# Expert stage of a two-block layer: hidden rows turned by VectorE in 32x32 blocks, places spread by one product, sums stored in 2 or 4 KB pieces

## Chip, core and metric

The kernel runs on one core of one Trainium2 chip. A core has five engines that run beside each other: TensorE (PE, with its weight loads as PEld), VectorE (DVE), ScalarE (ACT), GpSimd (POOL) and SyncE (SP, which here only issues loads). 16 DMA engines move data between DRAM and the on-chip memory. The metric is the device time of one execution in microseconds (us), the median over runs; less is better.

## What is computed

A first block (attention of two kinds, then a mixture of experts) and a second block (differential attention and retention), for 512 tokens of 1024 float32 values. Only the mixture of experts is touched by the change. Cut to what matters it is

```python
logits = (hf @ router_w + router_b)                  # 512 tokens, 32 experts
top_val, top_idx = lax.top_k(logits, 4)              # each token goes to 4 experts
gate = jax.nn.softmax(top_val, axis=-1)
# for the rows (tokens) of one expert e:
u = hf[toks] @ w1[e] + b1[e]                         # w1[e]: 1024 x 2048
g_, lin = u[:, :1024], u[:, 1024:]
g_ = jnp.minimum(g_, 7.0); lin = jnp.clip(lin, -7.0, 7.0)
y = ((lin + 1.0) * g_ * jax.nn.sigmoid(1.702 * g_)) @ w2[e] + b2[e]   # w2[e]: 1024 x 1024
out = segment_sum(y * gate)                          # back to the 512 tokens
```

All weights are float32, so one expert's are 8 MB of w1 and 4 MB of w2, and all 32 experts are read whatever the routing.

## The kernel before

**Experts and rows.** The 32 experts are taken in an order that is computed at run time: expert 0 first, the others so that their row counts fit a fixed list of capacities, `QUADS` = 3, 3, 2, 3, 2, 3, 3, 2, 3, 4, ... in units of 32 rows. It has 11 twos, 19 threes and 2 fours, 87 quads in all, and ends with a two. Rows over the capacity would go through an extra loop (`over`), which these inputs do not enter.

**Weights.** They pass through `ring`, 12 slots of 1 MB in on-chip memory. Slots 0 to 7 take the eight 1 MB pieces of an expert's w1 (L891), slots 8 to 11 the four of its w2 (L895). SP issues a slot's next load as soon as TensorE signals that it has used the slot (`w1_used`, `w2_used`, `main.y`), in the order w1 of expert n+1, then w2 of expert n. In both cases a partition receives 8 KB that lie together in DRAM. Partition after partition these runs follow each other in DRAM without a gap.

**TensorE**, for n = 0 to 32: the first layer of expert n (`first_layer`, L1427), then the second layer of expert n-1 (`second_layer`, L1444). Both use tiles of 32 stationary columns, so four products with different column groups run beside each other. The first layer's output is laid out by quads: bank g holds quad g, and the partition group c of 32 holds the columns 256c to 256c+255 of its gate half and of its linear half. Between the eight pieces of the first layer stand small jobs: `turn_hidden` of expert n-1 (L1416, after pieces 1 and 2; for n = 1 after 5 and 6), `spread` (L1399, after 3), `indices` (L1391, after 4) and `turn_rows` (L1408, after 5 and 6; for n = 1 after the whole first layer).

**Hidden values.** DVE adds the bias (L1838) and computes the gated product `act_t` (L1841 to L1849). TensorE turns it in 128x128 blocks (L1416), ACT copies the result out of PSUM to `actT` (L1169), and the second layer reads `actT` as its stationary side. The second layer computes 256 output columns per product and per quad.

**Places.** `indices` gathers a row's token number, gate and validity as one row of `meta`; `spread` repeats this over the four partition groups, one product per quad, and DVE makes the DRAM row numbers of it (`targets`, L1824 to L1828).

**Sums.** ACT scales each quad's 128x256 result by the gates into `ybuf` (L1176), and POOL adds it to `expert_sums` in DRAM with an indirect accumulating DMA (`put`, L1038). One DMA covers a quad, 128 pieces of 1 KB: one piece for each partition. Rows without a token are added to junk rows. The tokens' rows are fetched by another indirect DMA, 4 KB a row (`fetch`, L1029). The last expert's result does not go to DRAM: TensorE adds it to the residual by a product with a one-hot matrix (L1537), and DVE accumulates (L1920).

## Time and profile before

| | us |
|---|---|
| median of 3 runs | 1993.21 |
| the runs | 1987.38 to 1993.46 |
| the profiled execution, its own time | 1989.01 |
| its span, first to last instruction | 1987.3 |
| first product of the expert stage starts at | 519.8 |
| last product of the second layer ends at | 1586.6 |

The profile shows busy time per engine, waits with what ended them, the chain of work that ended last, and the DMA packets by queue. q1 is the queue of SP's loads, q0 that of POOL's indirect DMAs, and q8 the fetching of instructions. A "share of 16 engines" is the packets' time over 16 times the length of the stretch. Packets of one engine overlap slightly, so the sum can pass 100%.

### The profile page before, as it was taken

What the parts mean: (1) busy time and instruction counts of PE and PEld (TensorE: products, weight loads), DVE (VectorE), ACT (ScalarE), POOL (GpSimd) and SP (SyncE); (2) the same over time, 40 slices, a digit from 0 to 9 for tenths busy, and PEclk for the clock granted to TensorE, in tenths of its full rate; (3) what the DMA queues carried; (4) which work ended last, traced back from release to release, by engine and by line L of the source; (5) the groups of instructions that cost most, each with busy time, mean ns of one, the idle gap of its engine ahead of it and who ended that gap; (6) DMA issues with size and microseconds to landing.
All of it is one profiled execution on the core that took longest, in us unless ns stands there. A gap on an engine that the chain in (4) does not pass through costs nothing.

```text
span 1987.3 us, 37108 instructions
## 1 busy us (share of the span) xinstructions
PE 1885.2 (95%) x15662; PEld 976.1 (49%) x15662; DVE 675.7 (34%) x1755; ACT 371.4 (19%) x821; POOL 192.3 (10%) x237
## 2 busy tenths in 40 slices
PE   5999999998899999999999998999999869989989
PEld 4486755753444444444444433334343434855754
DVE  6436957422322121212131212112122153186140
ACT  2214732431111111111111101111011122062010
POOL 1020000000011111021112121112120100000000
PEclk9979999999899999999999999999999989999999
DMA  9721322422599999999999999999999782100001
GB/s 300 227 85 53 97 85 85 170 80 69 201 340 389 395 398 402 399 393 389 396 401 393 399 394 406 394 390 368 401 390 406 286 291 70 58 1 0 1 0 43
DMA packets 144751, 498.99 MB, mean 251 GB/s; under 512 B 20786, under 2 KB 89512, under 8 KB 95432
## 3 DMA queue, kind: packets, MB, share of 16 engines
q1 hardware_dynamic: 122192, 464.81, 60.6%
q0 software_dynamic: 16448, 22.69, 5.4%
q10 hardware_dynamic: 5944, 9.09, 1.3%
q8 instruction: 126, 2.06, 0.4%
q14 instruction: 41, 0.34, 0.0%
HBM read 481.08 MB, written 17.96 MB: 251 GB/s over the span
## 4 chain that ended last, share of the span: by engine, by line
PE 78%; DMA 10%; DVE 8%; issue 2%; ACT 1%; SPq 1%; ACTq 0%; DVEq 0%
PE bank L1427 26%; PE bank L1444 12%; PE bank L395 10%; DMA ring<-in_exp_w_dram 9%; PE bank L403 8%; PE bank L799 6%; DVE arena L661 1%; PE bank L1416 1%; PE bank L1408 1%; PE bank L770 1%; PE bank L580 1%; DVE arena L630 1%; PE bank L379 1%; PE bank L1391 1%; DVE arena L746 1%
## 5 line engine op out<-in xcount | busy, mean ns | idle before, releaser
L1427 PE MATMUL bank<-ring,arena 128*32 128x512 f32 x5568 | 646.1, 599 | 14.0 <-DMA ring<-in_exp_w_dram 11.8
L1427 PEld LDWEIGHTS bank<-ring,arena 128*32 128x32 f32 x5568 | 163.6, 110 | 327.3 <-issue 294.6
L1444 PE MATMUL bank<-ring,arena 128*32 128x256 f32 x5568 | 307.9, 379 | 7.3 <-DMA ring<-in_exp_w_dram 5.9
L1444 PEld LDWEIGHTS bank<-ring,arena 128*32 128x32 f32 x5568 | 181.7, 110 | 140.8 <-issue 22.0
L395 PE MATMUL bank<-hT,ring 128*128 128x512 f32 x448 | 210.2, 621 | 13.2 <-DVE hT L776 7.5
L1824 DVE COPY arena<-bank 128x12 f32<-128x12 f32 (+2 forms) x32 | 5.4, 170 | 558.0 <-PE bank L1391 543.8
L1038 POOL DMA_INDIRECT expert_sums<-arena,dst_r x85 | 131.7, 1550 | 403.5 <-ACT arena L1176 387.0
L403 PE MATMUL bank<-ring,hT 128*128 128x256 f32 (+1 forms) x768 | 156.4, 363 | 0.0
L395 PEld LDWEIGHTS bank<-hT,ring 128*128 128x128 f32 x448 | 87.6, 199 | 119.1 <-issue 115.8
L403 PEld LDWEIGHTS bank<-ring,hT 128*128 128x128 f32 x768 | 135.6, 190 | 18.4 <-issue 2.4
L1838 DVE TENSOR_TENSOR arena<-bank,arena 128x512 f32<-128x512 f32 x87 | 54.9, 683 | 191.0 <-PE bank L1427 191.0
L799 PE MATMUL bank<-hT,ring 128*128 128x512 f32 x256 | 113.0, 595 | 1.4 <-ACT hT L821 1.4
L1158 ACT ACTIVATE arena<-bank 128x384 f32<-128x384 f32 (+2 forms) x64 | 29.4, 461 | 363.0 <-PE bank L1408 362.8
L1029 POOL DMA_INDIRECT arena<-h_rows,src_i x32 | 32.8, 1026 | 591.6 <-PE bank L1408 421.6
L799 PEld LDWEIGHTS bank<-hT,ring 128*128 128x128 f32 x256 | 47.7, 190 | 57.9 <-issue 56.0
L630 DVE SCALAR_TENSOR_TENSOR arena<-ring,vecs,arena 128x256 f32<-128x256 f32 x154 | 74.6, 484 | 3.5
L580 PE MATMUL bank<-arena 128*128 128x128 f32 x480 | 71.6, 282 | 0.5
L1176 ACT ACTIVATE arena<-bank,arena 128x256 f32<-128x256 f32 x85 | 34.5, 473 | 196.5 <-PE bank L1444 196.5
L1169 ACT ACTIVATE arena<-bank 128x384 f32<-128x384 f32 (+2 forms) x64 | 29.4, 461 | 220.4 <-PE bank L1416 220.4
L580 PEld LDWEIGHTS bank<-arena 128*128 128x128 f32 x480 | 61.4, 192 | 4.9 <-ACT arena L598 3.7
L606 ACT ACTIVATE arena<-arena,mn 128x128 f32<-128x128 f32 (+3 forms) x96 | 53.8, 560 | 49.7 <-DVE mn L661 47.7
L1164 ACT ACTIVATE arena<-arena 128x768 f32<-128x768 f32 (+2 forms) x32 | 25.1, 786 | 167.1 <-DVE arena L1841 167.1
(335 smaller groups left out, 1612.5 us busy)
## 6 DMA issues: line engine op xcount, KB each, us to landing
ring<-in_exp_w_dram SPq DMA_DIRECT2D x384, 1024.0 KB, 24.0
ring<-in_ada_w_dram SPq DMA_DIRECT2D x24, 1024.0 KB, 12.0
ring<-in_w_in_dram SPq DMA_DIRECT2D x23, 1024.0 KB, 10.1
ring<-in_w_out_dram SPq DMA_DIRECT2D x8, 1024.0 KB, 5.1
expert_sums<-arena POOLq DMA_DIRECT2D x5, 512.0 KB, 4.7
arena<-in_x_dram ACTq DMA_DIRECT2D x1, 2048.0 KB, 13.1
ring<-in_w_in_dram SPq DMA_DIRECT2D x8, 256.0 KB, 4.7
h_rows<-arena ACTq DMA_DIRECT2D x4, 512.0 KB, 3.3
```

Source lines behind the costliest of these rows:

```text
L395: mm = pe.matmul(z[:, :], w, hT[:, k, :], start=(k == 0), stop=(k == ND - 1))
L403: mm = pe.matmul(z[:, n * wd:(n + 1) * wd], hT[:, k, i * P:(i + 1) * P], chunk(j["name"], j["part"])[:, k, j["col"]:j["col"] + wd], start= ...
L580: mm = pe.matmul(bank[6 + n % 2][:, 0:P], probT[n % 2][:, b * P:(b + 1) * P], st["v"](b), start=(b == 0), stop=(b == st["blocks"] - 1))
L606: act.activation(st["p"][:, 0:w], st["p"][:, 0:w], ACT.Exp, scale=-1.0, bias=mn[:, n % 4:n % 4 + 1], accum_out=ls[:, n % 4:n % 4 + 1]).the ...
L630: ins = dve.scalar_tensor_tensor(out=ada_sum[ch], in0=w, scalar=s, in1=ada_sum[ch], op0=ALU.mult, op1=ALU.add)
L799: mm = pe.matmul(bank[2 + n % 3][:, :], chunk(name, n // 2)[:, k, P * (n % 2):P * (n % 2) + P], hT[:, k, :], start=(k == 0), stop=(k == ND ...
L1029: pool.indirect_dma_start(xg[0:rows, :], None, h2_dram, bass.IndirectOffsetOnAxis(src_i[0:rows, 0:1], 0), bounds_check=S - 1, oob_is_err=F ...
L1038: pool.indirect_dma_start(y_quarters, bass.IndirectOffsetOnAxis(dst[:, g:g + 1], 0), ybuf[:, g, :], None, bounds_check=4 * (JUNK + CAP) - ...
L1176: act.activation(ybuf[:, g, :], bank[4 + g // 2][:, SW * (g % 2):SW * (g % 2 + 1)], ACT.Copy, scale=gate[:, g, 2:3]).then_inc(sg.y_ok, 1)
L1427: mm = pe.matmul(bank[g][QUAD * c:QUAD * (c + 1), :].rearrange("p (h n) -> p h n", h=2), rowsT[:, k, QUAD * g:QUAD * (g + 1)], w[:, :, SW ...
L1444: mm = pe.matmul(bank[4 + g // 2][QUAD * c:QUAD * (c + 1), SW * (g % 2):SW * (g % 2 + 1)], actT[:, j, g, QUAD * q:QUAD * (q + 1)], w[:, c, :],
L1838: ins = dve.tensor_tensor(u_in[:, g, :], bank[g][:, :], b1_rows, ALU.add)
```

## The change

TensorE no longer turns the hidden values, and ACT no longer copies them. DVE writes `act_t` with its columns regrouped (eight apart) and turns it in 32x32 blocks by one instruction for each expert, at the end of the gated product (`turn_hidden` on DVE). Since each block is turned inside its partition group, the second layer's contraction runs over other rows of w2 than before. So w2 is read with another pattern: partition p now gets rows 8p+2q and 8p+2q+1 for slot q, still 8 KB that lie together, but 32 KB from the next partition's.

The second layer's output is laid out differently. Two quads share 512 columns: partitions 0 to 63 hold the first 512 columns of 64 rows, partitions 64 to 127 the other 512. The third quad of a three takes 256 columns in a bank of its own. A four has one row of 1024 columns for each partition. So a row leaves in pieces of 2 KB (two quads), 1 KB (the third quad) or 4 KB (a four), and an expert has 1, 2 or 1 accumulating DMAs in place of 2, 3 or 4.

`spread` is one product in place of one per quad. `src_i` is now written before `meta`. Only `turn_rows` stays between pieces 5 and 6 for n = 1 too. The last expert's 16 one-hot products over 32 rows become 8 over 64 rows, signalled after each pair. DVE prepares the tables (`slot_row`, `slot_base`, `part_of`, `repl`) with 15 small instructions in place of 3.

```diff
-            w2_rows = exp_w2[0].rearrange("e (q p j) n -> p q e j n", p=P, j=2)
+            w2_rows = exp_w2[0].rearrange("e (p q j) n -> p q e j n", p=P, j=2)
...
-            def put(sg, n, before, dst, quads):
+            def put(sg, n, parts, puts, dst, quads):
                 pool.wait_ge(sg.dst, n)
-                for g in range(quads):
-                    pool.wait_ge(sg.y_ok, before + (g + 1))
-                    pool.sem_inc(waited_pool, 1)
-                    pool.indirect_dma_start(y_quarters, bass.IndirectOffsetOnAxis(dst[:, g:g + 1], 0), ybuf[:, g, :],
-                                            None, bounds_check=4 * (JUNK + CAP) - 1, compute_op=ALU.add)\
-                        .then_inc(sg.put, 16)
-                pool.wait_ge(sg.put, 16 * before + 16 * quads)
+                pool.wait_ge(sg.y_ok, parts + PARTS[quads])
+                if quads == 4:
+                    put_rows(sg, y_dram, (JUNK + CAP) - 1, dst[:, 0:1], ybuf)
+                else:
+                    put_rows(sg, y_halves, 2 * (JUNK + CAP) - 1, dst[:, 0:1], ybuf[:, 0:2 * SW])
+                if quads == 3:
+                    put_rows(sg, y_quarters, 4 * (JUNK + CAP) - 1, dst[:, 1:2], ybuf[:, 2 * SW:3 * SW])
+                pool.wait_ge(sg.put, 16 * puts + 16 * PUTS[quads])
                 pool.sem_inc(sg.free, 1)
...
-            def hidden_in(sg, n, quads):
-                for j in range(2):
-                    act.wait_ge(sg.at, n + (j + 1))
-                    act.activation(actT[:, j, 0:quads, :], bank[6 + j][:, 0:P * quads].rearrange("p (g t) -> p g t", t=P),
-                                   ACT.Copy).then_inc(sg.at_ok, 1)
+            PIECES = {2: [(0, 512, 0)], 3: [(0, 512, 0), (512, SW, 1)], 4: [(0, 512, 0), (512, 512, 0)]}
...
-                for g in range(quads):
-                    mm = pe.matmul(bank[4][:, 16 + 4 * g:20 + 4 * g], repl[0:rows, g, :], meta[0:rows, :], start=True,
-                                   stop=True)
-                mm.then_inc(sg.rows, 1)
+                pe.matmul(bank[4][:, 16:16 + cols], ident[:, :] if quads == 4 else repl[0:rows, :],
+                          meta[0:rows, 0:cols], start=True, stop=True).then_inc(sg.rows, 1)
...
-                        for g in range(quads):
-                            for c in range(4):
-
-                                mm = pe.matmul(bank[4 + g // 2][QUAD * c:QUAD * (c + 1), SW * (g % 2):SW * (g % 2 + 1)],
-                                               actT[:, j, g, QUAD * q:QUAD * (q + 1)], w[:, c, :],
+                        for b, c, g, col, width in SECOND[quads]:
+                            mm = pe.matmul(bank[b][QUAD * c:QUAD * (c + 1), 0:width], actT[:, g, 2 * q + j, :],
+                                           w[:, col:col + width], start=(q == 0 and j == 0), stop=(q == 3 and j == 1))
...
-                    if n >= 2 and k in (1, 2):
-                        turn_hidden(main, n, QUADS[n - 1], [k - 1])
-                    if n == 1 and k in (5, 6):
-                        turn_hidden(main, n, QUADS[n - 1], [k - 5])
...
-                    pe.wait_ge(main.at_ok, 2 * n)
+                    pe.wait_ge(main.at_ok, n)
...
-            for j in range(2):
-                for g in range(QUADS[-1]):
-                    for c in range(4):
-                        rows = slice(QUAD * c, QUAD * (c + 1))
-                        mm = pe.matmul(bank[2 * c + j][:, :], y_last[rows, g, P * j:P * (j + 1)], hot_last[rows, g, :],
-                                       start=(g == 0), stop=(g == QUADS[-1] - 1))
+            for t in range(4):
+                for h in range(2):
+                    rows = slice(HD * h, HD * (h + 1))
+                    mm = pe.matmul(bank[4 * h + t][:, :], y_last[rows, P * t:P * (t + 1)], hot_last[rows, :], start=True,
+                                   stop=True)
                 mm.then_inc(last_t, 1)
...
+            def turn_hidden(sg, n, quads):
+
+                dve.wait_ge(sg.act, n)
                 if sg is main and n >= 2:
-                    dve.wait_ge(main.at, 2 * (n - 1))
+                    dve.wait_ge(main.y, n - 1)
+                dve.transpose(actT[:, 0:quads, :, :].rearrange("p g b t -> p (g b t)"),
+                              act_t[:, 0:quads, :].rearrange("p g n -> p (g n)")).then_inc(sg.at_ok, 1)
```

The order of the instructions shows where this lands. Names: `landedK` tells that slot K has arrived, `m_act` that the gated product is ready, `m_y` that a second layer is done, `m_y_ok` that ACT has taken a result out. First TensorE, in the first layer of the third expert (two quads), from its second piece on, before:

```order
L1427 MATMUL bank<-ring,arena 32x512 [waits landed1]
L1427 MATMUL bank<-ring,arena 32x512 x7
L1416 MATMUL bank<-ident,arena 128x128 [waits m_act]
L1416 MATMUL bank<-ident,arena 128x128 x2
L1427 MATMUL bank<-ring,arena 32x512 [waits landed2]
L1427 MATMUL bank<-ring,arena 32x512 x7
L1416 MATMUL bank<-ident,arena 128x128 [waits m_act]
L1416 MATMUL bank<-ident,arena 128x128 x2
L1427 MATMUL bank<-ring,arena 32x512 [waits landed3]
L1427 MATMUL bank<-ring,arena 32x512 x7
L1399 MATMUL bank<-meta,arena 128x4 [waits m_meta,m_y_ok]
L1399 MATMUL bank<-meta,arena 128x4 x2
```

and the same place now:

```order
L1424 MATMUL bank<-ring,arena 32x512 [waits landed1]
L1424 MATMUL bank<-ring,arena 32x512 x7
L1424 MATMUL bank<-ring,arena 32x512 [waits landed2]
L1424 MATMUL bank<-ring,arena 32x512 x7
L1424 MATMUL bank<-ring,arena 32x512 [waits landed3]
L1424 MATMUL bank<-ring,arena 32x512 x7
L1404 MATMUL bank<-arena 128x8 [waits m_meta,m_y_ok]
```

The turning products (L1416) with their wait are gone, and three spreading products have become one. Then VectorE, at the end of the same expert's gated product, before:

```order
L1844 SCALAR_TENSOR_TENSOR arena<-arena 128x512 [waits m_g,dv]
L1849 TENSOR_TENSOR arena<-arena 128x512 [waits m_at,m_sig,dv]
L1893 TENSOR_LOAD order_i
L1893 ISA x2
L1832 ISA
L1832 COPY arena<-arena 128x16
```

and now:

```order
L1853 SCALAR_TENSOR_TENSOR arena<-arena 128x512 [waits m_g,dv]
L1858 TENSOR_TENSOR arena<-arena 128x2x32x8 [waits m_sig,dv]
L1866 STREAM_TRANSPOSE arena<-arena 128x512 [waits m_y,m_act]
L1910 TENSOR_LOAD order_i
L1910 ISA x2
L1841 ISA
L1841 COPY arena<-arena 128x16
```

A transpose has come in, with a wait for the second layer that reads `actT` (`m_y`); the bias work of the next expert stands behind it. Last POOL, at the first accumulating DMAs (two threes, then a two), before:

```order
L1038 DMA expert_sums<-arena,dst_r 2560x256 [waits m_dst,m_y_ok]
L1038 DMA expert_sums<-arena,dst_r 2560x256 [waits m_y_ok] x2
L1029 DMA arena<-h_rows,src_i 64x1024 [waits m_put,m_xt,m_src]
L1038 DMA expert_sums<-arena,dst_r 2560x256 [waits m_dst,m_y_ok]
L1038 DMA expert_sums<-arena,dst_r 2560x256 [waits m_y_ok] x2
```

and now:

```order
L1043 DMA expert_sums<-arena,dst_r 1280x512 [waits m_dst,m_y_ok]
L1043 DMA expert_sums<-arena,dst_r 2560x256
L1035 DMA arena<-h_rows,src_i 64x1024 [waits m_put,m_xt,m_src]
L1043 DMA expert_sums<-arena,dst_r 1280x512 [waits m_dst,m_y_ok]
L1043 DMA expert_sums<-arena,dst_r 2560x256
```

A three leaves in two DMAs in place of three, and both wait for the whole result.

## Rows read from the trace of the kernel before

**Rows 1.** The page: busy tenths, DMA share and rate in 40 slices.
```profile
PE   5999999998899999999999998999999869989989
...
DMA  9721322422599999999999999999999782100001
GB/s 300 227 85 53 97 85 85 170 80 69 201 340 389 395 398 402 399 393 389 396 401 393 399 394 406 394 390 368 401 390 406 286 291 70 58 1 0 1 0 43
```

**Rows 2.** Busy time in stretches of the stage; last columns clock, DMA share, GB/s.
```profile
core 0: us, PE busy (x) PEld busy (x) DVE busy (x) ACT busy (x) POOL busy (x), PEclk, DMA share, GB/s
...
580.00:1560.00 980.00, 965.30 (x11090) 402.37 (x11086) 208.39 (x460) 110.60 (x229) 155.95 (x110) 1.00 1.03 395
1140.00:1240.00 100.00, 90.64 (x1044) 37.87 (x1040) 19.20 (x46) 10.82 (x23) 15.54 (x11) 1.00 1.03 400
```

**Rows 3.** DMA view, 580 to 1560 us: packets, queues, issues with median us to landing.
```profile
DMA packets 65127, 386.78 MB, mean 395 GB/s; under 512 B 8034, under 2 KB 18431, under 8 KB 20178
...
q1 hardware_dynamic: 50446, 367.36, 92.8%
q0 software_dynamic: 14573, 17.81, 9.1%
q8 instruction: 88, 1.44, 0.6%
...
ring<-in_exp_w_dram SPq DMA_DIRECT2D x350, 1024.0 KB, 24.6
```

**Rows 4.** DMA view, 520 to 580 us.
```profile
q1 hardware_dynamic: 2358, 17.22, 77.4%
...
ring<-in_exp_w_dram SPq DMA_DIRECT2D x18, 1024.0 KB, 5.3
```

**Rows 5.** Waits, 586 to 1573 us: us in total, times, longest.
```profile
PE bank L1427 <- DMA ring<-in_exp_w_dram: 11.8, 13, 1.6
...
PE bank L1444 <- DMA ring<-in_exp_w_dram: 4.6, 7, 1.0
```

**Rows 6.** DMA view, 1052 to 1060 us: three accumulating DMAs beside the loads.
```profile
DMA packets 716, 2.97 MB, mean 372 GB/s; under 512 B 87, under 2 KB 391, under 8 KB 391
...
q0 software_dynamic: 351, 0.31, 24.4%
```

**Rows 7.** DMA view, 1600 to 1620 us: loads of w_in_2 in 1 KB pieces.
```profile
q1 hardware_dynamic: 6206, 6.27, 98.0%
```

**Rows 8.** The chain that ended last, 480 to 600 us: start, us, what.
```profile
517.47 1.13 PE bank L1399 x6
...
560.01 0.54 PE bank L1399 x4
...
566.74 0.56 PE bank L1416 x3
...
573.27 0.64 PE bank L1408 x8
```

**Rows 9.** Timeline around the end of the stage, 1560 to 1600 us.
```profile
1568.47 8.10 SPq L895 DMA_DIRECT2D ring<-in_exp_w_dram  x4
...
1584.69 1.93 PE L1444 MATMUL bank<-ring,arena 128*32 128x256 f32 x32 [1.26 <-DMA ring<-in_exp_w_dram]
1586.76 0.84 ACT L1195 ACTIVATE arena<-bank,arena 128x256 f32<-128x256 f32 x2 [8.81 <-PE bank L1444]
...
1587.74 3.71 PE L1537 MATMUL bank<-arena 32*128 32x512 f32 x32 [1.11 <-ACT arena L1195]
...
1589.87 5.36 DVE L1920 SCALAR_TENSOR_TENSOR resT<-bank,mod,resT 128x512 f32<-128x512 f32 x8 [19.76 <-PE bank L1537]
```

**Rows 10.** Groups of instructions in 500 to 1650 us: busy us, mean ns, idle before.
```profile
L1416 PE MATMUL bank<-ident,arena 128*128 128x128 f32 x174 | 37.5, 320 | 0.0
...
L1399 PE MATMUL bank<-meta,arena 96*128 96x4 f32 (+2 forms) x174 | 25.1, 258 | 0.0
...
L1833 DVE STREAM_TRANSPOSE arena<-arena 128x512 f32<-128x512 f32 x32 | 22.8, 712 | 1.1
```

**Rows 11.** Timeline of VectorE, 490 to 496 us.
```profile
495.57 0.68 DVE L1757 COPY arena<-bank 32x512 f32<-32x512 f32 x1 [4.61 <-PE bank L1360]
```

More of the change, by code:

```diff
@@ L78, in two_block_layer @@
     ROWS_BY = [QUAD * sum(QUADS[:n]) for n in range(NEXP + 1)]
-    PARTS_BY = [sum(QUADS[:n]) for n in range(NEXP + 1)]
+    PARTS, PUTS = {2: 1, 3: 2, 4: 2}, {2: 1, 3: 2, 4: 1}
+    PARTS_BY = [sum(PARTS[q] for q in QUADS[:n]) for n in range(NEXP + 1)]
+    PUTS_BY = [sum(PUTS[q] for q in QUADS[:n]) for n in range(NEXP + 1)]
     h2_dram = nc.dram_tensor("h2_rows", (S, D), F32, kind="Internal").ap()
```

138 lines of the change are left out of this document (74 added, 64 removed).

## The prediction, made before the changed kernel ran

> **What bounds the kernel now.** I read the 40 slices first [rows 1]. From slice 12 to 31 the DMA share is 9 in every slice, at 368 to 406 GB/s, and PE is at 9 nearly everywhere too. So two resources look full, and the question is which one sets the length. The windows sharpen it: over 980 us the DMA engines are busy 1.03 of the time, and PE for 965 us [rows 2]. The DMA view shows how much work is queued [rows 3, 4]. While the first two experts run, a 1 MB load lands 5.3 us after its issue, so hardly anything stands ahead of it. In the stage the median is 24.6 us. At 395 GB/s that is 24.6 x 395 / 1049 = about 9 of the 12 slots under way at once. A freed slot therefore joins a long queue, and freeing it sooner does not make it land sooner. PE waits for a load only 11.8 + 4.6 = 16.4 us in all [rows 5], because it started with a reserve of landed slots and uses it up: where the reserve is gone, from 1140 to 1240 us, PE is busy 90.6 of 100 us while the rate stays at 400 GB/s [rows 2]. My reading: **from about 586 to 1573 us the length is the DMA engines' work**. PE's work fits inside it with a few per cent to spare. Before 586 us the loads are paced by PE: the queue's share is 77.4% [rows 4].
>
> The sum is made against the profiled execution, 1989.0 us of its own time (span 1987.3). The median of the runs shown is 1993.2, 4.2 above it; I carry the difference over.
>
> **PE's saved work, inside the stage.** The turning products cost 37.5 us [rows 10], and they vanish. The spreading products cost 25.1 us for 174 records; 64 are left, so some 16 us go. The second layer streams the same columns with fewer weight loads, which I put at nothing. That is about 53 us of PE, the largest number in this sum, and I value it at nothing between 586 and 1573 us: the loads cover it. What is late next is the load that PE already waited for. If that cover were gone, the 53 us would count in full.
>
> **The start, before the queue is long.** Here PE sets the issue of the loads, so its savings count. The spread before the first product takes 1.13 us for 6 records [rows 8] and becomes 2 records, about 0.4 us: -0.7. The one inside the first expert falls likewise, -0.4, and the third expert's, 0.54 us for 4 records, -0.2. For n = 1 two turnings of 0.56 us and the 0.64 us of row turning behind the layer become two row turnings of half 0.64 and some overhead, 0.36 each: 1.76 - 0.72 = 1.0. Together **-2.3 us**. The 12 more table instructions on DVE come before a wait of 4.61 us for the router's product [rows 11]. At the 0.2 us that small ones take they need 2.4 us and are hidden; without that wait they would cost it.
>
> **The accumulating DMAs.** This is the term that counts, since it is DMA work inside the DMA-bound stretch. In the window with three of them q0 holds 24.4% of 16 engines for 8 us, 31.2 us of one engine [rows 6]. It has 391 - 87 = 304 pieces of 1 KB beside tiny ones, so one piece costs **0.103 us**. Over the stage: 18431 - 8034 = 10397 such pieces [rows 3], 1068 of the 1427 us of one engine that q0 takes there (9.1%). The rest is 20178 - 18431 = 1747 fetched rows of 4 KB, 0.206 us each. SP's loads take 92.8% x 980 x 16 = 14551 us for 367.36 MB, in 8 KB pieces 0.324 us each, **0.041 us a KB**. So a 1 KB piece costs 2.5 times its share of the stream, and something in it is fixed.
>
> How many merge: every two and three but the last expert makes one 2 KB piece of two 1 KB pieces in each partition (10 + 19 experts), and two fours make one of four. That removes 29 + 2 x 3 = 35 pieces for each of 128 partitions, 4480 in all, 280 per DMA engine. What a removed piece saves is not in the trace. Bounds from the nearest rows: if cost goes with bytes, nothing (a 2 KB piece costs 0.206); if the second KB costs what a KB of the stream costs, 0.103 - 0.041 = 0.062. I see no reason for less than nothing. A fetched row of 4 KB has 0.206 - 4 x 0.041 = 0.042 fixed, the nearest row with a larger indirect piece, and I take that: 0.042 x 280 = **-11.5 us**, between 0 and -17.
>
> A rule of the Trainium skill speaks against this term (DMA: Bandwidth & Descriptors, Specifications): pieces of 512 B and more already run at line rate. By it the merged pieces save nothing, and the term would be 0. Rows 6 and 7 disagree with it so far: 1 KB pieces cost 0.103 us when they accumulate, and 98.0% x 20 x 16 / 6206 = 0.051 us as plain loads of w_in_2, against 0.041.
>
> **Instruction fetching.** q8 takes 0.6% of the stage, 5.9 us [rows 3]. Some 4900 of about 25000 instructions there vanish (4352 records of the second layer, 348 of turning, 220 of spreading): **-1.1 us**, between 0 and -1.1.
>
> **The pattern of w2.** Same bytes, same 8 KB runs, but now 32 KB apart. No row shows such a load. The bound on the good side is 0. On the bad side stand the nearest strided loads, w_in_2's, at 0.051 us a KB [rows 7]: 64 KB per engine and slot x 0.010 = 0.64 us, for 31 x 4 slots = +79 us. I take **0**: those pieces are eight times shorter, and that is reason enough for their price. The Trainium skill has a rule that warns here (DMA: Bandwidth & Descriptors, Latency and other measured facts): large power-of-two pitches between partitions cost rate, 207 against 214 GB/s at 512 KB and half the rate at 4 MB. It gives nothing for 32 KB. By its mildest figure, 3% on w2's loads, the sum would rise by about 10 us.
>
> **VectorE and the waits added.** A transpose of 128x512 takes 0.71 us [rows 10], so 0.7 to 1.4 us an expert on an engine that is busy 208 of 980 us [rows 2]. It stands behind a wait for the second layer of the expert before. Queued behind it are the next expert's bias work and then the places, which need `indices` after piece 4 of the next first layer, so they lose nothing; TensorE needs the turned values a whole first layer later. The strided read of the gated product is the one unknown, and at double price it adds 1 us where 10 or more are free. All of that: 0. POOL's first DMA now waits for ACT's last copy, half a microsecond, with a whole expert's time before the next need: 0.
>
> **The end.** The last w2 slot is asked for when the second layer before is done, and PE waits for its landing at 1584.69 [rows 9]; the saved turning there is hidden by that. Then: one ACT copy in place of two (0.84, -0.2), and DVE may start after the first pair of products in place of half of 3.71 us, about 0.9 in place of 2.0 us, and then needs 5.36 us in any case: -1.1. Together **-1.3**, at worst +0.8 if the pairs do not run beside each other.
>
> **Sum.** -2.3 - 11.5 - 1.1 + 0 - 1.3 = **-16.2 us**: 1989.0 becomes 1972.8, and against the median 1993.2 it is **1977.0**. With both ends of the put term, and the noise of the runs, this case spans 1969 to 1986.
>
> **Rivals.**
>
> 1. *The put pieces save nothing* (bytes alone count, or the pieces are cut to 1 KB again on the way). For: at 0.103 us they might be moved twice, in and out, 0.082 us by the stream's price, and then only 0.021 a piece is fixed: 5.9 us. Against: the fetched row. Left are start, fetching and end, -4.7: 1988.5, no change that can be told.
> 2. *The 32 KB pattern is slower* (ends on the other side). Place: the 124 w2 slots of the stage, which lie one after another in a full queue. Price: up to 0.64 us a slot; at a quarter of that +20, at the bound +79. It cancels the gain from 16.2 / 124 = 0.13 us a slot, 5% of one. For: nothing covers it, since the queue is the bound. Against: runs of 8 KB stay whole. At half the bound: 1977 + 40 = 2017.
> 3. *PE is the bound after all*. For: PE's 9s and only 16.4 us of waits [rows 1, 5]. Then the 53 us count, and the stage shrinks until the DMA engines stop it. Against: 24.6 us to landing and a share of 1.03. It needs loads that run faster when asked earlier; the stretch of full reserve use shows 400 against a mean of 395 GB/s [rows 2], 1.3% or 13 us of it. Time: 1977 - 13 = 1964.
>
> **Chances.** Forecast 0.62, rival 1 0.20, rival 2 0.11, rival 3 0.07. A measurement of this kernel can tell about 0.3%, 6 us. Faster by more: the forecast but for its weak edge, rival 3 and a few cases of rival 1, 0.72; within: 0.17; slower: 0.11. The range takes the forecast's span, rival 1 and the upper half of rival 3: 1966 to 1993.
>
> **What would show it.** q0's share in the stage falls from 9.1% to about 8%, with 19 x 128 = 2432 pieces of 1 KB in place of 10880 in all. SP's median to landing rises towards 30 us, and PE's waits for loads from 16 to about 16 + 53 - 13 = 55 us, at an unchanged clock of 1.00. An 8 KB piece of the loads still costs 0.324 us; if it costs more, rival 2 holds. If a 2 KB piece costs 0.2 us, rival 1. If PE's waits stay at 16 us while the stage shrinks by far more than 13 us, rival 3. The first product starts some 0.7 us earlier, and the last accumulation on DVE follows the last copy sooner. The forecast is wrong altogether if the stage's length does not follow the DMA work.

## The result, and the profile after

The changed kernel takes 1976.7 us (median of 5 runs, 1975.5 to 1978.1), the kernel before 1991.7 us beside it (5 runs, 1987.4 to 1993.5). The ratio is 0.9932, 95% interval 0.9921 to 0.9942: 0.7% faster, 15.0 us between the medians and 13.5 us by the ratio. Forecast were 1977.0 us and faster by more than 0.3%. The figure is met more closely than its working deserves, which is luck. The profiled executions differ by 13.6 us (1989.01 and 1975.45 us of their own time; spans 1987.3 and 1973.6), where the sum said 16.2, and several terms of the sum were wrong in both directions.

The page of the changed kernel: spans and busy time, the 40 slices, the queues. The lines answer to [rows 1].

```profile
span 1973.6 us, 31966 instructions
...
PE 1840.0 (93%) x13186; PEld 871.5 (44%) x13186; DVE 717.9 (36%) x1795; ACT 336.4 (17%) x723; POOL 138.2 (7%) x204
...
PE   6999999998899999999998988999989769989989
...
DMA  9721322422499999999999999999999782100001
GB/s 305 226 86 46 105 86 86 171 81 69 184 358 395 395 396 408 404 392 398 398 400 394 402 396 406 399 401 379 403 395 411 287 281 78 43 1 1 0 1 43
```

In tenths hardly anything moves: the DMA row keeps its 9s, and PE's has four 8s and a 7 in slices 12 to 31 in place of two 8s. The busy time tells more, 1840.0 us against this row of the page of before:

```profile
PE 1885.2 (95%) x15662; PEld 976.1 (49%) x15662; DVE 675.7 (34%) x1755; ACT 371.4 (19%) x821; POOL 192.3 (10%) x237
```

The DMA view of the same stretch as [rows 3], 580 to 1560 us:

```profile
DMA packets 60419, 387.25 MB, mean 395 GB/s; under 512 B 7516, under 2 KB 9820, under 8 KB 15407
...
q1 hardware_dynamic: 50539, 368.04, 92.4%
q0 software_dynamic: 9792, 17.91, 8.4%
q8 instruction: 70, 1.15, 0.5%
...
ring<-in_exp_w_dram SPq DMA_DIRECT2D x351, 1024.0 KB, 28.3
```

9820 - 7516 = 2304 pieces of 1 KB are left of 10397, q0 has gone from 9.1 to 8.4%, and a load lands 28.3 us after its issue, not 24.6. The window ends at a fixed time, though, so the rates say little on the length. For that I use one measure in all kernels below, **S**: from the start of the first product of the first expert to the end of the last product of the last second layer. In the changed kernel these are two rows of the timeline:

```profile
518.92 13.27 PE L1424 MATMUL bank<-ring,arena 128*32 128x512 f32 x96
...
1570.81 1.92 PE L1447 MATMUL bank<-ring,arena 128*32 128x512 f32 x16 [0.31 <-DMA ring<-in_exp_w_dram]
```

S is 1570.81 + 1.92 - 518.92 = 1053.8 us. Before it is 1584.69 + 1.93 - 519.80 = 1066.8 us, with the end from [rows 9] and this start:

```profile
519.80 12.82 PE L1427 MATMUL bank<-ring,arena 128*32 128x512 f32 x96
```

So of the 13.7 us of span, 0.9 lie ahead of the first product, 13.0 in S, and behind it 0.2 are given back.

The waits of PE, 586 to 1573 us (us in total, times, longest), against [rows 5]:

```profile
PE bank L1424 <- DMA ring<-in_exp_w_dram: 27.3, 41, 1.7
PE bank L1447 <- DMA ring<-in_exp_w_dram: 22.2, 22, 2.7
```

They rose from 16.4 to 49.5 us, where the prediction said about 55. PE did 45 us less and waits 33 us more.

### The profile page after: what moved, and what is told of

Read it like the earlier page. It is cut to its first block, busy times and chain, and to the rows that moved or that the text cites. A ratio compares the mean times of both kernels' runs of the same rounds, so it can differ in the third digit from the quotient of the medians.

```text
span 1973.6 us, 31966 instructions
## 1 busy us (share of the span) xinstructions
PE 1840.0 (93%) x13186; PEld 871.5 (44%) x13186; DVE 717.9 (36%) x1795; ACT 336.4 (17%) x723; POOL 138.2 (7%) x204
## 4 chain that ended last, share of the span: by engine, by line
PE 64%; DMA 22%; DVE 7%; SPq 3%; issue 2%; ACT 1%; ACTq 0%; DVEq 0%
DMA ring<-in_exp_w_dram 21%; PE bank L1424 18%; PE bank L400 10%; PE bank L1447 9%; PE bank L408 8%; PE bank L804 6%; SPq L896 2%; DVE arena L666 1%; SPq L900 1%; PE bank L585 1%; PE bank L775 1%; PE bank L384 1%; DVE arena L751 1%; DVE arena L635 1%; PE bank L1412 1%
## 5 line engine op out<-in xcount | busy, mean ns | idle before, releaser
L1424 PE MATMUL bank<-ring,arena 128*32 128x512 f32 x5568 | 637.5, 598 | 30.0 <-DMA ring<-in_exp_w_dram 27.3
L1424 PEld LDWEIGHTS bank<-ring,arena 128*32 128x32 f32 x5568 | 169.5, 110 | 383.3 <-issue 319.4
L1447 PE MATMUL bank<-ring,arena 128*32 128x512 f32 (+1 forms) x3392 | 310.1, 518 | 23.5 <-DMA ring<-in_exp_w_dram 22.2
L400 PE MATMUL bank<-hT,ring 128*128 128x512 f32 x448 | 211.1, 624 | 13.2 <-DVE hT L781 7.5
L1447 PEld LDWEIGHTS bank<-ring,arena 128*32 128x32 f32 x3392 | 108.9, 110 | 227.3 <-issue 170.1
L1833 DVE COPY arena<-bank 128x8 f32<-128x8 f32 (+1 forms) x32 | 5.3, 165 | 363.1 <-PE bank L1397 353.2
L1172 ACT ACTIVATE arena<-bank 128x384 f32<-128x384 f32 (+2 forms) x64 | 29.4, 460 | 575.4 <-PE bank L1412 575.2
L1043 POOL DMA_INDIRECT expert_sums<-arena,dst_r x50 | 77.6, 1552 | 446.4 <-issue 414.0
L1866 DVE STREAM_TRANSPOSE arena<-arena 128x768 f32<-128x768 f32 (+2 forms) x32 | 28.9, 903 | 147.9 <-PE bank L1447 147.8
L1187 ACT ACTIVATE arena<-bank,arena 128x512 f32<-128x512 f32 (+1 forms) x52 | 29.4, 606 | 215.6 <-PE bank L1447 215.6
## 6 DMA issues: line engine op xcount, KB each, us to landing
arena<-in_x_dram ACTq DMA_DIRECT2D x1, 2048.0 KB, 12.5
```

Of the source, the lines that this page charges most:

```text
L400: mm = pe.matmul(z[:, :], w, hT[:, k, :], start=(k == 0), stop=(k == ND - 1))
L1043: pool.indirect_dma_start(to, bass.IndirectOffsetOnAxis(index, 0), rows, None, bounds_check=limit, compute_op=ALU.add).then_inc(sg.put, 16)
L1424: mm = pe.matmul(bank[g][QUAD * c:QUAD * (c + 1), :].rearrange("p (h n) -> p h n", h=2), rowsT[:, k, QUAD * g:QUAD * (g + 1)], w[:, :, SW ...
L1447: mm = pe.matmul(bank[b][QUAD * c:QUAD * (c + 1), 0:width], actT[:, g, 2 * q + j, :], w[:, col:col + width], start=(q == 0 and j == 0), st ...
```

## The experiments

Each was timed beside runs of the kernel before (medians 1988.9 to 1990.1 us), so the ratios are what compares. S comes from each one's trace. Each S is that of one execution. Two of the kernels change what should cost nothing, and their S moved by 0.3 and 1.1 us, so I take S to tell about 1 us. A difference of two ratios has 3 to 4 us to each side, so whatever below is smaller than that rests on S and the waits, and not on the times.

| kernel | median us | ratio to before, 95% | S, us | S against |
| --- | --- | --- | --- | --- |
| before | 1991.7 | 1 | 1066.8 | |
| w2 pitch in the kernel before | 1990.1 | 1.0001 (0.9992 to 1.0011) | 1067.1 | before +0.3 |
| changed | 1976.7 | 0.9932 (0.9921 to 0.9942) | 1053.8 | before -13.0 |
| changed, 1 KB pieces | 1981.1 | 0.9956 (0.9942 to 0.9970) | 1058.0 | changed +4.2 |
| changed, one set of idle transposes | 1978.7 | 0.9942 (0.9926 to 0.9958) | 1055.7 | changed +1.9 |
| changed, three sets | 1980.7 | 0.9948 (0.9931 to 0.9966) | 1059.2 | changed +5.4 |
| changed, 1 KB and three sets | 1982.0 | 0.9964 (0.9952 to 0.9976) | 1060.9 | changed +7.1 |
| changed, empty places left out | 1966.3 | 0.9882 (0.9867 to 0.9898) | 1045.2 | changed -8.6 |
| changed, no third groups' sums | 1963.2 | 0.9867 (0.9851 to 0.9884) | 1041.3 | changed -12.5 |
| changed, accumulating DMAs twice | 2033.4 | 1.0222 (1.0205 to 1.0239) | 1109.1 | changed +55.3 |
| changed, no accumulating DMAs | 1926.7 | 0.9685 (0.9669 to 0.9701) | 1004.4 | changed -49.4 |
| changed, w1 loads asked for later | 1983.4 | 0.9972 (0.9961 to 0.9982) | 1061.5 | changed +7.7 |
| changed, PE's start as before | 1979.1 | 0.9953 (0.9936 to 0.9971) | 1054.4 | changed +0.6 |
| changed, product in plain order | 1977.0 | 0.9940 (0.9925 to 0.9955) | 1054.9 | changed +1.1 |

### The w2 pattern

In the kernel before:

```diff
-            w2_rows = exp_w2[0].rearrange("e (q p j) n -> p q e j n", p=P, j=2)
+            w2_rows = exp_w2[0].rearrange("e (p q j) n -> p q e j n", p=P, j=2)
```

> The kernel before with the one line of the w2 pattern taken from the changed kernel: each 8 KB run of a slot now starts 32 KB after that of the partition before it, not 8 KB. The products then meet w2's rows in another order than the activations, so the sums are not the reference's; bytes, slots and order of work are the same. Forecast (the pitch costs nothing): 1992 us, within 3 us of the kernel before, and an 8 KB piece keeps its 0.32 us. Rival 2 (the pitch costs rate): 0.13 us or more for each of 124 slots, so 2008 us or more, up to 2070.

1.0001, with the interval a tenth of a per cent to each side. Its DMA view from 580 to 1560 us stands beside [rows 3]: the same share, the same rate.

```profile
DMA packets 65107, 386.88 MB, mean 395 GB/s; under 512 B 8031, under 2 KB 18389, under 8 KB 20145
...
q1 hardware_dynamic: 50453, 367.47, 92.8%
```

Rival 2 is out: an 8 KB run costs the same whether the next one starts 8 or 32 KB further.

### The pieces back to 1 KB

```diff
-                if quads == 4:
-                    put_rows(sg, y_dram, (JUNK + CAP) - 1, dst[:, 0:1], ybuf)
-                else:
-                    put_rows(sg, y_halves, 2 * (JUNK + CAP) - 1, dst[:, 0:1], ybuf[:, 0:2 * SW])
-                if quads == 3:
-                    put_rows(sg, y_quarters, 4 * (JUNK + CAP) - 1, dst[:, 1:2], ybuf[:, 2 * SW:3 * SW])
+                for g in range(quads):
+                    put_rows(sg, y_quarters, 4 * (JUNK + CAP) - 1, dst[:, g:g + 1], ybuf[:, SW * g:SW * (g + 1)])
...
+                for g in range(4 if quads == 4 else 2):
+                    ins = dve.tensor_scalar(dst[:, g:g + 1], dst_f[:, 0:1], 4.0 if quads == 4 else 2.0, float(g),
+                                            ALU.mult, ALU.add)
```

> The changed kernel, but its sums leave in 1 KB pieces as before: a pair of quarters by two DMAs to addresses one quarter apart, a four by four. The same bytes go to the same rows; VectorE works out the further addresses with 1 to 5 small instructions an expert, which other work hides. 4480 pieces more, 280 for each DMA engine. The forecast's own price (0.042 us a piece) says 1976.7 + 11.5 = 1988 us. The trace of the changed kernel, where a 2 KB piece takes clearly less than two of 1 KB but more than a 1 KB piece and 1 KB of the stream, says 0.026 x 280 = 7 us: 1984 us. Rival 1 (bytes alone count): 1977 us. If the whole of the change's gain were here, 1992 us.

Slower by 0.9956 / 0.9932 = 1.0024, 4.8 us with about 3.4 to each side, and S is 4.2 us longer. Merging is worth 4 to 5 us, not 11.5. Why is told by one expert with two groups of rows, whose sums leave between 1102 and 1110 us in both traces (DMA view, 8 us). First the changed kernel, then the one with 1 KB pieces:

```profile
DMA packets 524, 3.04 MB, mean 380 GB/s; under 512 B 57, under 2 KB 57, under 8 KB 185
...
q0 software_dynamic: 144, 0.26, 17.7%
```
```profile
DMA packets 642, 3.02 MB, mean 378 GB/s; under 512 B 58, under 2 KB 305, under 8 KB 305
...
q0 software_dynamic: 263, 0.25, 19.6%
```

185 - 57 = 128 pieces of 2 KB hold an engine for 17.7% x 8 x 16 = 22.7 us, 0.177 us each. 305 - 58 = 247 pieces of 1 KB hold one for 25.1 us, 0.1016 each. A merge saves 2 x 0.1016 - 0.177 = 0.026 us. The second KB costs 0.075 us, near the price of rival 1 for a KB moved in and out (0.082), and not the 0.041 + 0.021 of my choice, which came from a fetched row that is moved once. The 280 merges should give 7 us by that; the clock shows 4 to 5, with 7 inside the interval of the times but above what S says.

### TensorE's saved work given back

One set, and with `range(3)` three:

```diff
+                    if n >= 3 and k in (1, 2):
+                        for _ in range(1):
+                            for g in range(QUADS[n - 1]):
+                                pe.transpose(bank[5 + k][:, P * g:P * (g + 1)], ident[:, :], ident[:, :])
```

> The changed kernel with the turning products' work given back to TensorE and nothing else: from the fourth expert on, as many 128x128 transposes of the identity as before stood after pieces 1 and 2 of each first layer, into banks that are free there, for nobody. About 35 us of TensorE, no transfer. Forecast (the DMA engines set the stage): PE's waits for loads fall from 49 to about 14 us and the time stays at 1977 us, up to 1980. Rival 3 (PE is the bound): 1977 + 35 = 2012 us.

> As the kernel with one set of idle transposes from the fourth expert on, but with three sets: about 105 us of TensorE. It asks where the cover ends. Forecast: the waits for loads, 49 us, are used up, and the rest counts: 1977 + 105 - 49 = 2033 us, somewhat more where the slack is not in the same place as the work. Rival 3 (all of PE's work counts): 2082 us. If the DMA engines had far more slack left than their share says: under 2020 us.

I had priced the transposes at what the turning products cost. Here they are the groups below (first one set, then three; 586 to 1573 us), back to back and cheaper:

```profile
L1488 PE MATMUL bank<-ident 128*128 128x128 f32 x158 | 30.0, 293 | 0.0
```
```profile
L1488 PE MATMUL bank<-ident 128*128 128x128 f32 x474 | 64.5, 279 | 0.0
```

All of PE is busy 1895.5 us with three sets against 1840.0: 55.5 us more, not the 105 of the expectation, so its 2033 us had no footing. Its waits for loads went from 49.5 to 24.2 us with one set and to 1.6 with three:

```profile
PE bank L1424 <- DMA ring<-in_exp_w_dram: 11.8, 17, 1.6
PE bank L1447 <- DMA ring<-in_exp_w_dram: 12.4, 14, 2.4
```
```profile
PE bank L1424 <- DMA ring<-in_exp_w_dram: 1.6, 1, 1.6
```

So 55 us of work cost 5.4 us of S, and 30 us cost 1.9. By the times alone they are 3 and 2 us with 4 to each side, which does not rule out nothing. Rival 3 (all of it counts) is out by far. That it is not nothing either rests on S and on what follows. In the kernel before, PE's waits stood at 16.4 us, between these two. Where the work counts can be seen from 1320 to 1380 us, where PE never waits. Windows of before, changed, and three sets (busy times, then clock, DMA share, GB/s):

```profile
1320.00:1380.00 60.00, 60.00 (x724) 26.28 (x716) 13.36 (x31) 6.98 (x14) 11.79 (x9) 1.00 1.02 373
```
```profile
1320.00:1380.00 60.00, 60.00 (x587) 19.96 (x582) 15.53 (x32) 5.54 (x10) 6.71 (x5) 1.00 1.02 387
```
```profile
1320.00:1380.00 60.00, 60.00 (x574) 21.95 (x570) 14.13 (x30) 4.49 (x8) 3.60 (x3) 1.00 1.01 366
```

And the loads issued there, median us to landing at the end of the row, in the same order:

```profile
ring<-in_exp_w_dram SPq DMA_DIRECT2D x22, 1024.0 KB, 19.3
```
```profile
ring<-in_exp_w_dram SPq DMA_DIRECT2D x23, 1024.0 KB, 24.6
```
```profile
ring<-in_exp_w_dram SPq DMA_DIRECT2D x21, 1024.0 KB, 16.2
```

PE is busy all the time in all three, a load lands sooner after its issue than in the stage as a whole, and the rate is 373, 387 and 366 GB/s, against 395. I read it so: PE frees the slots slowly, the queue is short, and in such stretches PE sets the issue, as at the start. The share of the DMA engines hides this, at 1.01 to 1.02, since the packets take longer there. The loads' rows of the same 60 us, before and with three sets:

```profile
q1 hardware_dynamic: 2904, 21.13, 90.5%
```
```profile
q1 hardware_dynamic: 2824, 20.58, 90.1%
```

An 8 KB piece takes 90.5% x 60 x 16 us / (21.13 MB / 8192 B) = 0.337 us before and 0.344 with three sets, where it takes 0.324 over the stage. 60 us at 387 in place of 373 are 2.2 us. These windows are fixed in time and the kernels are not at quite the same load in them. Counted by the loads (in the traces' packets, from the end of the 264th 1 MB load of the stage's weights to that of the 312th), the kernel before loses 3.2 us to the changed one there, and the one with three sets 2.6.

### Both

The edits of the two kernels above, 1 KB pieces and three sets.

> The changed kernel with its sums in 1 KB pieces and with three sets of idle transposes from the fourth expert on (64.5 us busy, 55 us more of TensorE in all): in the stage it has the DMA work and the TensorE work of the kernel before, give or take 2 us. Alone the pieces gave 4 us and the transposes 4 us. If both count beside each other, 1976.7 + 8 = 1985 us, and 1990 - 1985 = 5 us are left for what it does not undo: the start, the end and the fetching of instructions. If only the larger of the two counts, since the one hides the other: 1981 us, and 9 us are still unexplained.

S is 7.1 us longer, of 4.2 + 5.4 = 9.6 apart: they mostly add. Beside the 1 KB pieces the three sets cost 1060.9 - 1058.0 = 2.9 us and not 5.4; that a busier DMA queue hides more of PE would fit and is not shown. It leaves 13.0 - 7.1 = 5.9 us of S for what it does not undo (start, fetching, the third expert's turning).

### The accumulating DMAs twice, and not at all

Twice, with `more` a view of a second array of the same shape:

```diff
+                for where in (to, more):
+                    pool.sem_inc(waited_pool, 1)
+                    pool.indirect_dma_start(where, bass.IndirectOffsetOnAxis(index, 0), rows, None, bounds_check=limit,
+                                            compute_op=ALU.add).then_inc(sg.put, 16)
```

Not at all:

```diff
-                pool.sem_inc(waited_pool, 1)
-                pool.indirect_dma_start(to, bass.IndirectOffsetOnAxis(index, 0), rows, None, bounds_check=limit,
-                                        compute_op=ALU.add).then_inc(sg.put, 16)
+                pool.sem_inc(sg.put, 16)
```

> The changed kernel with every accumulating DMA issued twice, the second time into a second array of sums that nobody reads (it is filled with zeros beside the first, long before the experts). It prices these DMAs by the clock on the wall. In the trace of the changed kernel they hold a DMA engine for (3712 x 0.176 + 2432 x 0.101 + 256 x 0.33) / 16 = 61 us. If the whole busy time of a piece counts, as the prediction's sum had it: 1977 + 61 = 2038 us. Leaving out the empty places and merging the pieces both gave only about 0.6 of the busy time that they took away; if that is the rule, 1977 + 37 = 2014 us. If the bytes alone counted (23 MB at 395 GB/s): 1977 + 55 = 2032 us with the share of the loads unchanged.

> The changed kernel without its accumulating DMAs (the sums of 31 of the 32 experts are missing). 61 us of DMA engine time go. At the whole busy time the stage would shrink until TensorE's 49 us of waits are used up: 1977 - 49 = 1928 us. At 0.6 of it: 1977 - 37 = 1940 us, with some 12 to 15 us of waits left. If TensorE bounds earlier than its waits say: above 1945 us.

Doubled they cost 1.0222 / 0.9932 = 1.0292, 57 us (S: 55.3 for 61 us of engine time). Removed they give 50 us (S: 49.4), with PE's waits down to 10.7 (its rows from 500 to 1600 us, two layers):

```profile
PE bank L1445 <- DMA ring<-in_exp_w_dram: 5.5, 6, 2.2
PE bank L1422 <- DMA ring<-in_exp_w_dram: 5.2, 9, 1.2
```

This is the strongest evidence that the stage's length is DMA work: transfers into an array that nobody reads lengthen it by nine tenths of their engine time, and taking the real ones away gives back eight tenths. The 0.6 of the expectation fell.

### Leaving out the empty places, and an even removal

```diff
-                                        compute_op=ALU.add).then_inc(sg.put, 16)
+                                        oob_is_err=False, compute_op=ALU.add).then_inc(sg.put, 16)
...
-                    put_rows(sg, y_halves, 2 * (JUNK + CAP) - 1, dst[:, 0:1], ybuf[:, 0:2 * SW])
+                    put_rows(sg, y_halves, 2 * JUNK - 1, dst[:, 0:1], ybuf[:, 0:2 * SW])
```

and the same for the 1 KB and 4 KB pieces. The second kernel drops the DMA of the third group instead:

```diff
-                if quads == 3:
-                    put_rows(sg, y_quarters, 4 * (JUNK + CAP) - 1, dst[:, 1:2], ybuf[:, 2 * SW:3 * SW])
```

> The changed kernel, but its accumulating DMAs leave out the places that hold no token: the limit on their addresses ends ahead of the spare rows of the sums, as the fetching of rows leaves them out already. The 31 experts whose sums leave this way have 85 x 32 = 2720 places, of which some 2000 hold a token; 720 fall away, with two pieces of 2 KB at 0.176 us or four of 1 KB at 0.101 each. That is 720 x 0.38 / 16 = 17 us of the DMA engines. If the stage is theirs: 1976.7 - 17 = 1960 us, and PE's waits for loads fall from 49 to about 32 us. If a piece that is left out still costs the 0.02 us that seem fixed in it, 1961 us. If the DMA engines do not set the length, or dropped pieces cost as much as written ones: 1977 us.

> The changed kernel without the 1 KB accumulating DMAs of the 19 experts with three groups of rows (their third groups' sums are missing); the 2 KB and 4 KB ones stay. 2432 pieces of 0.103 us go, 15.7 us of the DMA engines, as evenly from all 128 partitions as they lay. Leaving out the empty places took away 16.0 us but gave only about 10, and there the pieces all go from the last rows of each group of 32, which may leave some DMA engines relieved and others not. If that unevenness is the reason, an even removal gives nearly all, as doubling the pieces did (57 of 61 us): 1977 - 14 = 1963 us. If 1 KB pieces lie partly beside other packets of the same engine and so cost the wall less than their busy time wherever they are: 1977 - 9 = 1968 us.

Leaving out the empty places keeps the whole computation and beats both kernels: 1966.3 us, 0.9882 (0.9867 to 0.9898) of the kernel before, 10 us under the changed one. The q0 rows of the two pages, empty places left out first:

```profile
q0 software_dynamic: 11408, 19.80, 4.2%
```
```profile
q0 software_dynamic: 8672, 20.19, 4.2%
```

Both hold the engines for 4.2% of the span, and the changed kernel's q0 holds 5.0%, so both took away the same engine time, some 16 us. They took away much the same pieces, too: by the packet counts of the pages the skipping leaves out 1996 of the 2432 pieces of 1 KB and 381 of the 3968 larger ones. The third groups are four fifths empty. The even removal gave 12.5 us of S, the other 8.6. The difference is larger than S scatters; the times alone (1963.2 and 1966.3, intervals overlapping) do not settle it. That some DMA engines are relieved and others not fits, and is not shown: the trace has no engine numbers. The Trainium skill (DMA: Bandwidth & Descriptors, The descriptor swizzle) says of a 1 MiB transfer to 128 partitions that each engine serves two groups of four partitions, 32 apart. If that held for these DMAs, empty places at the end of every group of 32 rows would always relieve the same engines; nothing here tests it.

### Loads asked for later

```diff
-                    sp.wait_ge(w1_used, 8 * (n - 1) + k + 1)
+                    sp.wait_ge(w1_used, 8 * (n - 1) + min(k + 4, 8))
```

> The changed kernel, but SyncE asks for a w1 slot's next load three pieces later than the slot is free (at the latest at the layer's end), some 8 us. Nothing else changes. Forecast: a freed slot joins a long queue, and freeing it sooner does not make it land sooner; so the median from issue to landing falls from 28 to about 20 us and the time stays within 3 us of 1977. If the rate depends on how many loads stand in the queue (which would be how TensorE's saved work counts): 5 us or more longer, 1982 or above.

It cost 0.9972 / 0.9932 = 1.0040, 8 us, more than the 3 that I allowed. SyncE's first loads after the first expert's, in the changed kernel and here:

```profile
524.51 46.17 SPq L896 DMA_DIRECT2D ring<-in_exp_w_dram  x16
```
```profile
531.68 40.45 SPq L896 DMA_DIRECT2D ring<-in_exp_w_dram  x16
```

The first reload is 7.2 us later, and S is 7.7 longer. From there on the landings stay at that distance and it does not grow over 30 experts with the same lateness each. So in the full queue it is free, as forecast; at the start each us that a load is late is a us of the end. I had overlooked that the edit reaches the start too.

### TensorE's start as before

```diff
+                    if n in (1, 2) and k in ((1, 2) if n == 2 else (5, 6)):
+                        for _ in range(QUADS[n - 1]):
+                            pe.transpose(bank[6 + (k - 1) % 2][:, 0:P], ident[:, :], ident[:, :])
-                    if k in (5, 6) and n + 1 < NEXP:
+                    if k in (5, 6) and n + 1 < NEXP and n != 1:
...
+                if n == 1:
+                    turn_rows(main, 16 * (n + 2), QUADS[n + 1])
```

> The changed kernel with TensorE's work at the start as before: idle transposes stand where the turning products of the first two experts stood, and the row turning for the third expert stands behind the second first layer again. 2.2 us of TensorE between 560 and 593 us, nothing else. By the prediction's start term it counts in full while the queue is short: 1979 us. If the loads already set the pace there, 1977 us, since the landings do not move. The clock dip that the kernel before shows from 545 to 555 us is not expected to come back, since nothing ahead of it changes.

S moved by 0.6 us for 2.2 us of work. By the ratios the time is 4 us over the changed kernel's (2 by the medians), with 4 to each side, and in the profiled run the difference lies behind the stage. By S, PE's work at 560 to 593 us counts by a quarter or so, not in full; the 0.6 is inside the scatter of S.

### The product in plain order

```diff
-                dve.tensor_tensor(act_t[:, 0:quads, :].rearrange("p g (b f) -> p g f b", b=8), by_row(l_t), by_row(s_t),
-                                  ALU.mult).then_inc(sg.act, 1)
+                dve.tensor_tensor(act_t[:, 0:quads, :], l_t[:, 0:quads, :], s_t[:, 0:quads, :], ALU.mult)\
+                   .then_inc(sg.act, 1)
```

> The changed kernel with the gated product written in plain order, not each eighth value first (the hidden units then stand in another order than w2's rows, so the sums are not the reference's). Its mean falls from 1.38 us to about 0.88 us for 768 columns, and the 0.5 us an expert is hidden: 1977 us, as with it. If it were on the path, 32 x 0.5 = 16 us less: 1961 us.

The groups of 768 columns in the changed kernel and in plain order:

```profile
L1858 DVE TENSOR_TENSOR arena<-arena 128x768 f32<-128x768 f32 x17 | 25.7, 1511 | 0.6
```
```profile
L1858 DVE TENSOR_TENSOR arena<-arena 128x768 f32<-128x768 f32 x17 | 16.3, 958 | 0.6
```

0.55 us an expert go, and nothing is won (S +1.1, within its scatter). VectorE is off the path.

## Why the prediction came out right, step by step

**What bounds the kernel: right.** The stage's length follows the DMA work. Twice the accumulating DMAs cost 57 us, none gave 50, idle work on PE cost a tenth of itself or less.

**The accumulating DMAs: the mechanism right, the size wrong.** The step that failed is the price taken from a fetched row, "the nearest row with a larger indirect piece": -11.5 us was -4.2 in S (4.8 by the times). A row that is only fetched does not show what a second KB costs where the sum is read, added and written. The 1 KB row itself (0.103 us) with the stream's price taken twice gave 0.021 of fixed cost, and that was the right reading (0.026 measured). I had it as rival 1 and gave it 0.20. Rival 1's sign, a 2 KB piece at 0.2 us, did not come, and its end of the range, nothing at all, is wrong too.

**PE's saved work inside the stage: "nothing" was wrong.** The three sets of idle transposes cost 5.4 us of S for 55.5 us of PE, and 2.9 beside the 1 KB pieces. The change took away 45 us, 3 of them at the start; scaled to the other 42 that is an estimate of 2.2 to 4.1 us. The step that failed is "A freed slot therefore joins a long queue" as a statement on the whole stage: the median of 24.6 us hid stretches where 19.3 us and 373 GB/s showed that the queue was not full. The page has the same dip, 368 GB/s in the slice that begins at 27 x 49.7 = 1341 us [rows 1], and I did not ask about it. Rival 3, that all of it counts up to 13 us, was wrong in size.

**The start: -2.3 in the sum.** By 570 us PE was 3.9 us ahead, and by other rows than mine. I had read single pieces in [rows 8]; the long blocks beside them moved more. The 96 products that open the second expert's first layer, before and in the changed kernel (start, us, idle before):

```profile
547.80 12.20 PE L1427 MATMUL bank<-ring,arena 128*32 128x512 f32 x96 [2.06 <-issue]
```
```profile
546.93 10.51 PE L1424 MATMUL bank<-ring,arena 128*32 128x512 f32 x96 [2.06 <-issue]
```

The first product starts 0.9 us sooner (0.7 forecast). The spread inside the first expert saved 0.44, as forecast, but the 96 products ahead of it took 0.45 more at a clock just as low. The row turnings are half the size, as forecast. What I had not foreseen is the 1.7 us by which the block above is shorter (1.2 with the 0.45 taken off). The clock says why. Windows of the kernel before, then of the changed one (clock, DMA share and GB/s at the end):

```profile
545.00:550.00 5.00, 2.94 (x24) 0.85 (x20) 4.12 (x6) 0.84 (x1) 0.00 (x0) 0.84 1.02 345
550.00:555.00 5.00, 5.00 (x43) 1.68 (x39) 2.38 (x4) 0.00 (x0) 0.00 (x0) 0.82 0.49 152
```
```profile
545.00:550.00 5.00, 3.07 (x32) 1.19 (x36) 4.90 (x7) 0.85 (x1) 0.00 (x0) 1.00 0.98 342
550.00:555.00 5.00, 5.00 (x52) 1.82 (x48) 3.11 (x4) 0.00 (x0) 0.00 (x0) 1.00 0.76 283
```

Before, the granted clock falls from 2.4 towards 1.2 GHz for part of these 10 us, after PE has stood still for 2.06 us; in the changed kernel PE stands still as long and keeps 2.4 GHz. The dip is not bound to the old kernel: of the fourteen profiled executions the block takes 12.2 us in the kernel before, in its w2 variant and in the changed kernel with the product in plain order, and 10.5 in the changed kernel and its other variants. But that is both of the executions on the old side and one of the twelve on the changed side, so a part of the change in it is not ruled out. In the same three the 96 products ahead took 12.8, 12.9 and 12.1 us, in the other eleven 13.2 to 13.4, so what the dip costs net is less than 1.7. What decides it is open.

How much of the start reaches the end can be read from what the loads moved in the first 60 us after the first product. These are the rows of q1 in the kernel before, the changed one, and the one with 1 KB pieces and three sets, whose start is the changed kernel's (DMA view from 519.80, 518.92 and 518.75 us, 60 us each):

```profile
q1 hardware_dynamic: 2350, 17.16, 77.1%
```
```profile
q1 hardware_dynamic: 2488, 18.16, 80.8%
```
```profile
q1 hardware_dynamic: 2499, 18.24, 80.5%
```

The kernel before is 1.00 MB behind, 2.7 us at the stage's rate of 367.36 MB in 980 us. In the three variants whose start ran otherwise such a lag is still there at the end: against the changed kernel the plain product is 0.22 MB or 0.6 us behind and its S 1.1 us longer, the start given back 0.32 MB or 0.9 us and 0.6, the later loads 3.18 MB or 8.5 us and 7.7. So I take 2.7 us for the start in S, of which up to 1.2 hang on the clock. With the 0.9 ahead of S that is 3.6, where the sum had 2.3.

**Instruction fetching, -1.1.** q8 moved 1.15 MB in place of 1.44 in the window. Its effect was not tried alone.

**w2's pattern, VectorE, the waits: 0, and 0 it was**, by the experiments above. PE waited once, 1.2 us, for ACT's copy, at the very end and under a load's landing.

**The end: -1.3 was about 0.** The timeline of the changed kernel, against [rows 9]:

```profile
1572.87 0.69 ACT L1203 ACTIVATE arena<-bank,arena 128x512 f32<-128x512 f32 x1 [7.78 <-PE bank L1447]
1573.70 3.70 PE L1525 MATMUL bank<-arena 64*128 64x512 f32 x16 [0.96 <-ACT arena L1203]
...
1574.94 5.36 DVE L1937 SCALAR_TENSOR_TENSOR resT<-bank,mod,resT 128x512 f32<-128x512 f32 x8 [9.45 <-PE bank L1525]
...
1585.14 0.59 PE L1543 MATMUL bank<-ident 128*128 128x2 f32 x2 [7.74 <-issue]
```

From the last product of the stage to DVE's first accumulation are 2.2 us, 3.25 before: 1.0 of the forecast's 1.3. But the next product stands behind a wait that the profile calls issue. It starts 12.4 us after the stage's end against 13.0, so half of the 1.0 is lost there, and the products after it (5.59 us for the same 32 that took 5.18) and the code up to the next block lose the rest. The step that failed is "and then needs 5.36 us in any case": what came behind it was an instruction stream that did not start sooner.

**The sum.** 0.9 ahead of S. In S: 4.2 for the pieces and 2.2 to 4.1 for PE, but together no more than the 7.1 that both cost when given back, so 6.4 to 7.1; 2.7 for the start; up to 1.1 for fetching, which no run tried. Together 9.1 to 10.9 of 13.0. The rest, 2 to 4 us, I cannot assign. The pieces were 7 us too large in the sum, everything else in S some 6 too small, the end 1.5 too large: the errors nearly cancel, and that is luck. The prediction was also set against a median of 1993.2 us, where five runs give 1991.7, which took up the 1.2 us by which the difference was overrated.

## What to carry to other kernels

Where the DMA engines set the length, price every transfer by the share that its queue holds in a short window of its own, and price accumulating pieces from accumulating rows: their second KB costs about as much as moving it twice. A median of issue to landing speaks for the middle of the stage only; look for the stretches with the lowest rate and the shortest queue, since there the engine that frees the buffers still counts. The busy share of the DMA engines does not show them, the rate and the time of a piece do. Rows that are written for nobody can be left out by the limit of the indices; here that was worth more than merging the pieces.

## What the runs showed of the hardware

- An accumulating piece of 1 KB takes 0.102 us of a DMA engine, one of 2 KB 0.177.
- A piece whose index lies past the limit still appears as a tiny packet: with the empty places left out the page counts 22603 packets under 512 B, the changed kernel's 20226. The sums of an expert with three groups, in the changed kernel and with the empty places left out (10 us each):

```profile
DMA packets 748, 3.74 MB, mean 374 GB/s; under 512 B 83, under 2 KB 211, under 8 KB 339
...
q0 software_dynamic: 288, 0.39, 22.4%
```
```profile
DMA packets 787, 3.92 MB, mean 392 GB/s; under 512 B 206, under 2 KB 214, under 8 KB 341
...
q0 software_dynamic: 287, 0.27, 15.4%
```

  Of 128 pieces of 1 KB 8 are left, and 7.0% of 160 us go, 11.2 us of one engine for 120 pieces, 0.093 each: what is left out costs next to nothing.
- An 8 KB piece of a load takes 0.324 us where loads wait in line (24.6 us to landing), 0.337 and 0.344 where they land in 19.3 and 16.2 us, and 77.1% x 60 x 16 us / (17.16 MB / 8192 B) = 0.353 at the start of the kernel before (5.3 us).
- VectorE's product of 128x768 takes 1.51 us with its results written 128 B apart, 0.96 in plain order. The Trainium skill (SBUF — State Buffer, Door 1: The DMA port swizzle) says that SBUF has lines of 16 bytes and that an access which goes on to a new line pays for it; by that a step of 128 B must cost, and the trace agrees.
- Idle transposes of one matrix run at 64.5 / 474 = 0.136 us each in threes, where the turning products took 37.5 / 174 = 0.216 us [rows 10].
